# Modulation sums in column groups, values' bias on VectorE, head scores in row halves, one product a tile for the spatial bias, and pair loads of experts

## The reference, cut to what matters

```python
h = _ab_mixer(h, ...)                     # convolutions; model one, layer 1
h = _mlstm_mixer(h, ...)                  # layer 2: v = h @ w_v + b_v; per head scores = q @ k^T * decay
x = x + _rmsnorm(_swiglu(...), g)         # after each
ada = silu(c) @ w_ada + b_ada             # 6144 values a layer; for the first 2048 of layer 1 also from c_ctx
def modulate(h, shift, scale):
    return h * (1 + scale) + shift
```

## Time and profile before

| | us |
|---|---|
| median of 3 runs | 2027.43 (2024.94 to 2030.43) |
| the profiled execution | 2026.93 |
| its span | 2025.1 |

### The profile page before, as it was taken

The page is one execution under the profiler, slowest core; times in us unless marked ns, Lnnn a source line. Parts: engine busy times, 40 slices in busy tenths (PEclk is TensorE's granted clock), DMA queues, the critical chain, the costliest instruction groups (busy, mean ns, idle before and its releaser), DMA issues.

```text
span 2025.1 us, 25148 instructions
## 1 busy us (share of the span) xinstructions
PE 1966.2 (97%) x10326; PEld 1327.9 (66%) x10326; DVE 581.5 (29%) x1349; ACT 424.4 (21%) x961; POOL 13.1 (1%) x34
## 2 busy tenths in 40 slices
PE   8999999999999999999999999999999999999998
PEld 7798888957988888666454454445886445545544
DVE  3178541422565613323111011111233111111111
ACT  2440000222301101332221222122102122112212
POOL 1000000000001000000000000000000000000000
PEclk9998999989999999989999999999999999999999
DMA  9644677422456763213999999999534999999995
GB/s 333 204 167 175 282 273 287 167 84 83 148 225 283 304 234 137 104 42 109 428 429 429 428 428 428 429 428 427 223 131 174 428 428 428 429 428 428 428 429 226
DMA packets 51581, 591.25 MB, mean 292 GB/s; under 512 B 6305, under 2 KB 14761, under 8 KB 15794
## 3 DMA queue, kind: packets, MB, share of 16 engines
q1 hardware_dynamic: 51218, 588.09, 71.4%
q10 hardware_dynamic: 288, 2.10, 0.3%
HBM read 584.69 MB, written 1.05 MB: 289 GB/s over the span
## 4 chain that ended last, share of the span: by engine, by line
PE 66%; DMA 28%; DVE 4%; issue 1%; SPq 0%; ACT 0%; DVEq 0%
DMA ring<-in_w_up 27%; PE ps L436 24%; PE ps L1080 14%; PE ps L668 7%; PE ps L1177 2%; PE ps L711 2%; PE ps L495 2%; PE ps L1061 1%; DVE work L1701 1%; DMA ring<-in_w_ada 1%; PE ps L1067 1%; PE ps L583 1%; PE ps L462 1%; PE ps L526 1%; PE ps L511 1%
## 5 line engine op out<-in xcount | busy, mean ns | idle before, releaser
L1080 PE MATMUL ps<-ring,work 128*64 128x512 f32 x2048 | 451.2, 593 | 14.3 <-DMA ring<-in_w_up 14.2
L436 PE MATMUL ps<-h,ring 128*128 128x256 f32 x2064 | 455.9, 382 | 3.0 <-DVE h L1963 2.2
L436 PEld LDWEIGHTS ps<-h,ring 128*128 128x128 f32 x2064 | 393.2, 191 | 58.4 <-issue 4.0
L1080 PEld LDWEIGHTS ps<-ring,work 128*64 128x64 f32 x2048 | 149.9, 137 | 307.6 <-issue 289.6
L1361 ACT ACTIVATE work<-ps 128x512 f32<-128x512 f32 (+1 forms) x186 | 95.6, 520 | 711.7 <-PE ps L436 300.9
L1177 PE MATMUL ps<-ring,work 128*64 128x512 f32 x1024 | 226.8, 595 | 1.6 <-DVE work L2163 1.6
L1361 ACT ACTIVATE work<-ps,ada,scale_g 128x128 f32<-128x128 f32 x256 | 96.2, 456 | 400.4 <-PE ps L1061 400.4
L2154 DVE TENSOR_TENSOR work<-ps,work 128x512 f32<-128x512 f32 x30 | 20.8, 692 | 518.6 <-ACT work L1361 518.6
L1177 PEld LDWEIGHTS ps<-ring,work 128*64 128x64 f32 x1024 | 70.6, 137 | 133.7 <-issue 128.0
L668 PE MATMUL ps<-work,ring 128*128 128x256 f32 (+1 forms) x704 | 148.3, 373 | 3.9 <-DVE work L1878 3.9
L1701 DVE SCALAR_TENSOR_TENSOR work<-ring,silu_c,work 128x512 f32<-128x512 f32 x196 | 143.7, 754 | 5.1
(11 more groups left out here) (297 smaller groups left out, 1286.2 us busy)
## 6 DMA issues: line engine op xcount, KB each, us to landing
ring<-in_w_gate SPq DMA_DIRECT2D x64, 2048.0 KB, 15.0
ring<-in_w_up SPq DMA_DIRECT2D x64, 2048.0 KB, 17.3
ring<-in_w_down SPq DMA_DIRECT2D x64, 2048.0 KB, 12.3
ring<-in_w_ada SPq DMA_DIRECT2D x24, 2048.0 KB, 9.2
ring<-in_w_ff_gate SPq DMA_DIRECT2D x10, 2048.0 KB, 15.1
ring<-in_w_ff_up SPq DMA_DIRECT2D x10, 2048.0 KB, 13.7
ring<-in_w_ff_down SPq DMA_DIRECT2D x8, 2048.0 KB, 12.2
ring<-in_ml_w_in SPq DMA_DIRECT2D x6, 2048.0 KB, 10.0
```

Of the source, the lines that this page charges most:

```text
L436: last = mm(ps[:, b, 0:T], w[:, k, m * P:(m + 1) * P], rhs[:, k, :], start=(k == 0), stop=(k == nk - 1))
L1080: last = mm(ps[e * CAP:(e + 1) * CAP, j, :], xg[:, k, e * CAP:(e + 1) * CAP], w[e][:, k, :], start=(k == 0), stop=(k == last_k), skip_grou ...
```

## The change

- The start loads x, the first chunk and the first 16 columns of `vec` in parts (tiles 0 and 1; 2 and 3; 4 to 7), the second part issued once the first has landed. The other constants but `con` and `lru_w` are loaded before chunk 8. The spread of `glu` stands before chunk 6.
- Modulation sums: four pieces of `made` at a time are summed into four quarters of the partitions of bank 7, by a stationary of 32 columns of which one holds ones; 4 groups in the first feed-forward, 3 in the second; one copy, four transposes and 3 or 1 copies bring them to `ada`. `made` has six buffers. The last two chunks of `w_ada` are accumulated behind the loop. The down projection opens its banks one by one.
- The values' bias is added by DVE from 128 equal rows, `v_rows`; head scores are made for two heads in the two row halves; the spatial bias is one product over all 256 tokens.
- Experts' matrices are stored in pairs, so that each row of a pair is 32 KB, and loaded by one DMA of 4 MB a pair. The second gate load is split: its first half waits only for the first half of the first gate product. An unused chunk makes the first slot even.

```diff
+START = (0, 2, 4)
+START_DMAS = (48, 32, 16)
...
+        made = region(FT * T + 4 * T, MADE, CH)
+        ada_rows = made[:, 0, :]
...
+        v_rows = region(4096, D)
...
+        unused = len(chunks)
+        chunk(None)
...
+        ADA_GROUPS = (4, 3)
+        ADA_COPIES = (3, 1)
+        ADA_CHUNKS = ((1, 2, 4), (2, 4))
...
-            def ada_sums(l, c):
-                for w in range(conditions(l, c)):
-                    turn.take(S["ada_made"])
-                    b = stat_bank()
-                    for m in range(4):
-                        last = mm(ps[:, b, 2 * m:2 * m + 2], made[:, c % 2, w, m * P:(m + 1) * P], ones[:, 0:2],
-                                  start=True, stop=True)
-                    close_bank(b, last, tiles_act, S["ada_raw"])
+            def ada_group(l, i):
+                turn.take(S["ada_made"], GROUPS)
+                if i == 0:
+                    open_bank(7)
+                last_group = i == ADA_GROUPS[l] - 1
+                for g in range(GROUPS):
+                    last = mm(ps[QUAD * g:QUAD * g + QUAD, 7, :], one_hot(i, QUAD), made[:, (GROUPS * i + g) % MADE, :],
+                              start=(i == 0), stop=last_group, skip_group_check=True)
+                if last_group:
+                    close_bank(7, last, tiles_act, S["ada_rows"])
+                else:
+                    turn.give(last, S["ada_summed"])
+            def ada_turned(l):
+                turn.take(S["ada_rows"])
+                b = stat_bank()
+                for j in range(CH // P):
+                    last = nc.tensor.transpose(ps[:, b, j * P:(j + 1) * P], ada_rows[:, j * P:(j + 1) * P], ident)
+                close_bank(b, last, tiles_act, S["ada_raw"], reads=ADA_COPIES[l])
...
-                        if c and m == 0:
-                            ada_sums(l, 2 * c - 2)
-                            ada_sums(l, 2 * c - 1)
-                            if l and c == 4:
-                                sum_stats()
+                        if m == 1 and c in ADA_CHUNKS[l]:
+                            ada_group(l, ADA_CHUNKS[l].index(c))
+                        if m == 0 and l and c == 4:
+                            sum_stats()
...
+                    banks = [(state["bank"] + 1 + m) % 4 for m in range(4)]
...
+                            if k0 == 0:
+                                open_bank(banks[m])
...
+                        if c and k0 == 0:
+                            ada_group(l, ADA_GROUPS[l] - 1)
+                        if c and k0 == KT:
+                            ada_turned(l)
...
-                    mm(ps[:, b, :], h[:, k, t * P:(t + 1) * P], w[:, k, :], start=(k == 0), stop=False)
-                last = mm(ps[:, b, :], ones_row, rowv("v_b")[:, c * CH:(c + 1) * CH], start=False, stop=True)
-                close_bank(b, last, tiles_act, S["mv"])
+                    last = mm(ps[:, b, :], h[:, k, t * P:(t + 1) * P], w[:, k, :], start=(k == 0), stop=(k == KT - 1))
+                close_bank(b, last, tiles_dve, S["mv"])
...
-            def head_scores(n):
-                b = next_bank()
-                lo = 64 * (n % 2)
-                kk, qq = k_m[lo:lo + 64, n // 2, :], q_m[lo:lo + 64, n // 2, :]
-                mm(ps[:, b, 0:T], kk[:, 0:P], qq, start=True, stop=True)
-                close_bank(b, mm(ps[:, b, T:T + P], kk[:, P:T], qq[:, P:T], start=True, stop=True),
-                           tiles_dve, S["weighted"])
+            release(n, tiles_dve)
+            def pair_scores(n):
+                banks = [next_bank() for i in range(2)]
+                rows = [slice(64 * i, 64 * i + 64) for i in range(2)]
+                for i in range(2):
+                    mm(ps[:, banks[i], 0:T], k_m[rows[i], n // 2, 0:P], q_m[rows[i], n // 2, :], start=True, stop=True)
+                for i in range(2):
+                    close_bank(banks[i], mm(ps[:, banks[i], T:T + P], k_m[rows[i], n // 2, P:T], q_m[rows[i], n // 2, P:T],
+                                            start=True, stop=True), tiles_dve, S["weighted"])
...
-                if n + 2 < HEADS:
-                    head_scores(n + 2)
+                if n % 2 and n + 1 < HEADS:
+                    pair_scores(n + 1)
...
+                mm(ps[:, b, 0:T], selb[:, j, :], bsp[:], start=True, stop=False, skip_group_check=True)
                 for t in range(TT):
-                    mm(ps[:, b, t * P:(t + 1) * P], selb[:, j, :], bsp[:], start=True, stop=False,
-                       skip_group_check=True)
...
+                last.then_inc(e_["gate_half"], 1)
...
+            sp.dma_start(vec[:, 0:16], a["vec"][:, 0:16]).then_inc(start_loaded[0], 16)
+            for i, (k, end) in enumerate(zip(START, START[1:] + (KT,))):
+                if i == 1:
+                    sp.wait_ge(start_loaded[0], START_DMAS[0])
+                sp.dma_start(ring[:, 0, k * CH:end * CH].rearrange("p (k c) -> p k c", c=CH),
+                             chunks[0][0][:, k:end, :]).then_inc(start_loaded[i] if end < KT else slot_loaded[0], 16)
+            sp.dma_start(vec[:, 16:NVEC], a["vec"][:, 16:NVEC]).then_inc(vec_loaded, 16)
...
+                def load_pair(w, pair):
+                    arrived, slots = slots_of(w)
+                    sp.dma_start(slots.rearrange("p e c -> p (e c)"), weights[w][l, pair]).then_inc(arrived, 16)
+                for w in range(3):
+                    for e in range(2):
+                        sp.wait_ge(*released[first + 2 * w + e - RING])
+                    load_pair(w, 0)
...
+                    freed = e_["gate_full"], e_["up_full"], e_["down_done"]
+                    arrived, slots = slots_of(0)
+                    for part, half_freed in enumerate((e_["gate_half"], e_["gate_full"])):
+                        at = slice(part * SLOT // 2, (part + 1) * SLOT // 2)
+                        sp.wait_ge(half_freed, 1)
+                        sp.dma_start(slots[:, :, at], weights[0][l, 1].rearrange("p (e c) -> p e c", e=2)[:, :, at]).then_inc(
+                            arrived, 16)
+                    for w in (1, 2):
+                        sp.wait_ge(freed[w], 1)
+                        load_pair(w, 1)
+                    with sp.Fori(0, NEXP // 2 - 2) as i:
+                        for w in range(3):
+                            sp.wait_ge(freed[w], i + 2)
+                            load_pair(w, i + 2)
...
-                if n == 8:
+                if n == TAPS_SLOT + 1:
+                    spread_groups(rep_rec, rpad, T, S["rec_in"], rec_spread)
                     sp.wait_ge(S["lru_conv"], HTL)
                     spread_groups(rep_glu, cpad, REP, S["glu"], glu_spread)
-                if n == TAPS_SLOT + 1:
-                    spread_groups(rep_rec, rpad, T, S["rec_in"], rec_spread)
+                if n == 8:
+                    for dst, src in ((misc[32:33, 0:NROW], a["row"]), (misc[0:8, 0:SELS], a["sel"]), (gw[:], a["gate_w"]),
+                                     (rw[:], a["router_w"]), (wsp[:], a["w_sp"]), (bsp[:], a["b_sp"]),
+                                     (spread_rows[:], a["spread_rows"])):
+                        sp.dma_start(dst, src).then_inc(consts_loaded, 16)
                 load(n)
+                if n == ffn_last + RING:
+                    sp.dma_start(v_rows, a["v_rows"]).then_inc(vec_loaded, 16)
...
-                    ada_make(l, m // 2, m % 2)
+                    if m < FT - 2:
+                        ada_make(l, m // 2, m % 2)
...
+                for c in (FT // 2 - 1, FT // 2):
+                    for half in range(2):
+                        ada_make(l, c, half)
...
+            def value_out(c, t):
+                turn.give(V.tensor_tensor(v_m[:, t, c * CH:(c + 1) * CH], tile(), v_rows[:, c * CH:(c + 1) * CH], ALU.add), S["mv"])
+            value_out(0, 0)
```

More of the change, by code:

```diff
@@ L51 @@
 EH = 512
+MADE = 6
 CAP = 64
@@ L288, in build @@
         consts_loaded = sem("consts_loaded")
-        start_loaded = sem("start_loaded")
+        start_loaded = [sem(f"start_loaded_{i}") for i in range(3)]
+        vec_loaded = sem("vec_and_value_rows_loaded")
         ctx_loaded = sem("ctx_loaded")
@@ L345, in build @@
         ffn_chunks(0)
+        ffn_last = len(chunks) - 1
         for c in (0, 1, 2, 3, 4, 5):
@@ L368, in build, with arrivals, landed @@
         seam_rows = (HTL + 2 * HTL, KT - 1 + 2, KT - 3 + 2 * 3)
+        def arrivals(n):
+            for first in moe_first:
+                if 0 <= n - first < 3 * NEXP:
+                    return (1 + (n == first + RING)) * ((n - first) % 2 == 0)
+            return n != unused
+        def landed(n):
+            return 16 * sum(arrivals(m) for m in range(n % RING, n + 1, RING))
         def conditions(l, c):
             return 2 if l == 0 and c < 4 else 1
+        ADA_GROUPS = (4, 3)
+        ADA_COPIES = (3, 1)
+        ADA_CHUNKS = ((1, 2, 4), (2, 4))
         bank_of = {tiles_act: [], tiles_dve: []}
@@ L1027, in experts @@
                 first = moe_first[l]
```

(35 more changed lines are left out.)

202 lines of the change are left out of this document (95 added, 107 removed).

## The result

The changed kernel takes 1972.93 us (median of 4 runs, 1971.83 to 1975.89), the kernel before beside it 2028.93; the ratio is 0.9727, 95% interval 0.9705 to 0.9749. The forecast was 1978, range 1964 to 1992. The profiled execution took 1975.89 with a span of 1974.1, 51.0 us less than the 2025.1 of before.

A forecast was written before the change was run, and what follows sets the result against it. TensorE was taken to bound most of the kernel, the full DMA queues the expert stages. Start 7.6, feed-forwards 27.3, mLSTM and attention 8.4 and experts 6.0 sum to 49.3 us: 2027.4 to 1978 us, range 1964 to 1992.

The forecast's parts named there:

- The 1.1 at rec_conv: Start: 1.1 us gained at the wait for rec_conv's spread rows, at 52.88 us; ends 0 and 4.
- the first matmul at 5.4: Start: TensorE begins near 5.4 us instead of 9.36, as the first part is only 0.79 MB.
- The hole and its low clock: First feed-forward: TensorE's 4.2 us wait for VectorE goes, and the low clock from 166 to 176 with it, 4.0 us.
- the waits ahead of the down projections: Feed-forwards: waits of 1.6 and 2.3 us go, with chunks 10 and 11 behind the loop and banks opened singly: 3.9 us.
- four pairs save 3.4: mLSTM head scores: a pair in row halves costs 0.85 us, as one head did in series; four pairs save 3.4 us.
- The bias row: mLSTM values: the bias row product costs TensorE 1.06 us, four of them 4.2 us, which move to VectorE.
- rival E: Start keeps its 4 us, and with less one-row work the clock stays up in the mLSTM too: 1972 us; chance 0.08.
- Spatial gate: Spatial bias: eight products of 128 columns become four of 256, 0.2 us less each, 0.8 us.
- Pair loads: Experts: half as many DMAs with 32 KB rows save 0.1 to 0.2 us a pair; 4 us taken from 3 to 5.5.
- the split: Experts: the split second gate load starts 3.6 us earlier, gaining about 1.0 us a layer, 2.0 in all.
- some 3 to 7 ns: Experts' loads: the fixed part of a row's DMA time, from comparing 8 KB and 16 KB rows.
- Rival D: Early holes only move, as the queue sets rec_conv and glu or the clock falls anyway: 7.6 + 4.0 lost, 1990 us; chance 0.16.

The follow-up runs named there:

- e8: Changed kernel with all parts of x and the first chunk issued at once, nothing waiting for part 0: 1973.28 us, ratio 0.9728.

## Why the prediction was right, point by point

- **The start** (7.6; measured 7.0). The hole closed for its 4.3 (the convolution starts 5.3 earlier, of which 1.0 came from ahead), the clock gave 1.8 instead of 2.2, since 256 instructions take 13.95 at full clock and not 13.5. The 1.1 at rec_conv came out as 1.0, with a wait of 0.6 there and not of 1 to 3. Its first step failed, the first matmul at 5.4 (it was 6.55), and without effect: in e8 it comes 1.6 us later still and the mixer ends at the same 126.1. Against the second profile of before the start gains 6.1.
- **Feed-forwards** (27.3; 28.4). Groups took 1.00 for the 1.05 forecast. The second feed-forward, which had no hole, gains 9.2 us, and 12 sums less 3 groups and 4 transposes, with the wait of 2.3, come to 9.3. The hole and its low clock come and go together, 8.6 us in the experiment for 8.2 in the sum. For the waits ahead of the down projections I named VectorE's order and the banks together; opening the banks one by one suffices. What I missed is the wait of 0.8 for ACT at the second half when all banks are opened at once.
- **mLSTM** (7.6; 2.8 in the first profile). The step that failed is "four pairs save 3.4": three do, 2.5, since rows 11 show the third head's scores and I didn't look at the first two, which stand together. The bias row was right. The rest is mostly the clock: before had 10.2 us at half ahead of the first head, the profiled after 13.7, and a spell of 3.4 at 480 that the first profile of before lacks. Half of the two is 3.4 us, and 7.6 - 0.9 - 3.4 leaves 3.3; the last 0.5 no run places. I had rival E for a clock that stays up, and none for one that falls longer.
- **Spatial gate** (0.8; 3.6). The term was mis-sized, 1.4 at full clock, and the tiles came out of the low clock, which the sum left where it was.
- **Experts** (6.0; 9.3). Pair loads 7.1 for 4, the split 1.1 for 2.0; 0.9 of the rest lies between the layers, where the first profile of before has a spell at 1545 and that of after none. The term that was mis-sized is the fixed part of a row, "some 3 to 7 ns", from a window of 152 packets (rows 14): 0.24 us a pair, over 24 rows of each engine, would be 10 ns for each row that is saved. The sign was right; that the saving belongs to the rows and not to the loads is argued, not shown.

Rival D didn't come: the holes are gone and no other one took their place. That errors of -5, +3 and +3 us nearly cancel is luck; the range of 28 us was wide enough for each.

## What to carry to other kernels

A hole on the bounding engine costs more than its length when the clock falls with it (3.6 us of waiting cost 5.3 here, 6.6 us cost 8.6), so position an off-path producer's consumer one step later before making the producer faster. Before forecasting a small gain, list the stretches at half clock and what stands before them: their length changes by several us between executions of the same code, and only what is left with the low clock taken off can be compared. Narrow products are cheap by instruction, and here the clock fell where they stood together; and in the one profile where they were spread out a later spell took back what was won. Neighbours in different rows or columns of the array overlap by themselves.

## What the runs showed of the hardware

- The granted clock falls to half while TensorE is busy all the time: busy 6.80 of 6.80 us, with 16-column products ahead. Turned to 256 columns (8.2 us), or spread among 512-wide products (40.8 us), the same gates leave it at 1.00. The length of such a spell differs between executions of the same code, 3.4 or 6.8 us.
- Four 512-wide products in four column groups take 0.86 us, in one group 3.41, so the overlap is a full factor of 4.
- A product of one row by 512 columns, standing among full ones, costs 1.05 us at full clock, more than a full one of 128 rows (0.86).
- Rows of 32 KB are read at 432 GB/s, rows of 16 KB at 429 (110.63 and 109.71 MB in 256 us), with the share at 100.4 and 100.7%: no loss from the longer row, and at most 0.08 us for each DMA while the queue is full.
